# A decoder step on one core: sample state stored by GpSimd, key/value stores a stage later, modulation and last gating beside products, the sample tile in four column quarters

## The reference, cut to what matters

```python
mod = (c @ w_ada + b_ada)[:, None, :]
sh1, sc1, gt1, sh2, sc2, gt2 = jnp.split(mod, 6, axis=-1)
h = x * (1.0 + sc1) + sh1
(qkv_a, z_a, b_a, a_a, q_b, k_b, v_b, f_b, g_a, g_b) = _split_cols(h @ w_in, IN_SIZES)
...
o_a, ssm_new = _gdn_chunked(q_a, k_a, v_a, beta, g, ssm0.astype(f32), chunk)
...
merged = jax.nn.sigmoid(g_a) * (o_a @ w_ba) + jax.nn.sigmoid(g_b) * (o_b @ w_bb)
x = _layernorm(DEEPNORM_ALPHA * x + gt1 * (merged @ w_out), ln1_g, ln1_b)
h2 = x * (1.0 + sc2) + sh2
```

## Time and profile before

| | us |
|---|---|
| median of three runs | 1723.35 |
| lowest, highest | 1720.29, 1732.3 |
| profiled execution | 1724.44 |
| its span | 1722.4 |
| TensorE busy in the span | 1570.8 (91%) |
| VectorE, ScalarE, GpSimd busy | 610.7, 322.2, 300.4 |

### The profile page before, as it was taken

One profiled execution on the slowest core, in us unless ns is written; L12 is line 12 of the kernel. 1 busy time (PEld: TensorE's weight loads), 2 busy tenths in 40 slices (PEclk: granted clock), 3 DMA queues, 4 the chain that ended last, 5 costly groups with the idle time before them and its releaser, 6 DMA issues. The chain is left out here.

```text
span 1722.4 us, 20830 instructions
## 1 busy us (share of the span) xinstructions
PE 1570.8 (91%) x7950; PEld 896.8 (52%) x7950; DVE 610.7 (35%) x1254; ACT 322.2 (19%) x697; POOL 300.4 (17%) x328
## 2 busy tenths in 40 slices
PE   5998999999999995999889978999999999998966
PEld 2865766664467783877764433333433433343422
DVE  2001344343274543442457962331111111111128
ACT  1002222433232221222110210111111111111121
POOL 5000000000018993000000341111111111111100
PEclk9998999999999997999899989999999999999989
DMA  9312110112153214130933026899999999999865
GB/s 337 111 49 83 49 50 1 49 50 80 53 147 132 99 64 133 58 120 16 339 107 127 25 98 258 337 422 416 416 414 405 399 410 412 387 416 421 322 234 247
DMA packets 111678, 357.13 MB, mean 207 GB/s; under 512 B 36011, under 2 KB 36139, under 8 KB 85459
## 3 DMA queue, kind: packets, MB, share of 16 engines
q1 hardware_dynamic: 88582, 304.08, 46.0%
q0 software_dynamic: 14384, 35.89, 5.3%
q10 hardware_dynamic: 8614, 15.84, 2.7%
HBM read 330.70 MB, written 37.64 MB: 214 GB/s over the span
## 5 line engine op out<-in xcount | busy, mean ns | idle before, releaser
L1959 PE MATMUL bank<-arena 128*32 128x512 f32 (+2 forms) x1536 | 334.9, 618 | 27.5 <-DMA arena<-in_w_up 27.5
L1959 PEld LDWEIGHTS bank<-arena 128*32 128x32 f32 (+2 forms) x1536 | 119.6, 138 | 210.3 <-issue 207.7
L1967 PE MATMUL bank<-arena 128*32 128x512 f32 (+2 forms) x768 | 168.7, 598 | 0.7 <-DVE arena L2654 0.7
L2648 DVE TENSOR_TENSOR arena<-arena,bank 128x256 f32<-128x256 f32 x46 | 19.4, 422 | 329.5 <-ACT arena L2323 329.5
L429 PE MATMUL bank<-arena 128*128 128x272 f32 x512 | 123.6, 405 | 8.4 <-PEq L252 4.0
L1172 PE MATMUL bank<-arena 128*128 128x272 f32 x512 | 128.1, 398 | 2.3 <-DMA arena<-in_w_in 2.0
L1946 POOL DMA_INDIRECT expert_rows<-arena x46 | 46.4, 1009 | 480.2 <-PE bank L1952 416.0
L437 PE MATMUL bank<-arena 128*128 128x512 f32 (+4 forms) x384 | 124.3, 482 | 2.8 <-PEq L1744 2.7
L429 PEld LDWEIGHTS bank<-arena 128*128 128x128 f32 x512 | 100.5, 197 | 30.8 <-issue 6.8
L1967 PEld LDWEIGHTS bank<-arena 128*32 128x32 f32 (+2 forms) x768 | 54.9, 134 | 110.7 <-issue 109.8
L1172 PEld LDWEIGHTS bank<-arena 128*128 128x128 f32 x512 | 93.3, 190 | 25.8 <-issue 5.0
(11 more groups left out here) (443 smaller groups left out, 2064.0 us busy)
## 6 DMA issues: line engine op xcount, KB each, us to landing
arena<-in_w_gate SPq DMA_DIRECT2D x64, 1024.0 KB, 12.9
arena<-in_w_up SPq DMA_DIRECT2D x64, 1024.0 KB, 17.8
arena<-in_w_down SPq DMA_DIRECT2D x64, 1024.0 KB, 15.8
arena<-in_w_ada SPq DMA_DIRECT2D x12, 2048.0 KB, 10.4
arena<-in_w_in SPq DMA_DIRECT2D x11, 2048.0 KB, 9.4
arena<-expert_rows SPq DMA_DIRECT2D x8, 2048.0 KB, 26.7
gate_logits<-arena ACTq DMA_DIRECT2D x16, 272.0 KB, 2.8
arena<-gate_logits SPq DMA_DIRECT2D x8, 544.0 KB, 5.6
```

The source lines that it names most:

```text
L1959: mm = nc.tensor.matmul(out[rows].rearrange("p (a n) -> p a n", a=2), x[:, k, rows], gate_up_slot(n)[:, :, k, :], start=k == 0, stop=k == ...
L1967: mm = nc.tensor.matmul(out[rows, :], h[:, k, rows], down_slot(n)[:, k, 512 * half:512 * half + 512], start=k == 0, stop=k == 1)
```

## The change

- GpSimd, no longer SyncE, issues the stores of the sample state and outputs, the eight row moves and the load of branch B's weights, after its own recurrence. SyncE's list goes from slab 3 to slab 11 without a break.
- The six stores of keys, values and log values are issued in the next stage, behind the two history loads.
- `modulate(1)` runs in the projection stage; TensorE starts the first feature group with k = 0 to 3 of both halves, waits for it, and then takes k = 4 to 7.
- The gating of group m = 7 runs at the start of the output projection's stage; TensorE starts tile 0 with k = 0 to 6 of both halves, waits for `mT_last`, and then takes k = 7. ScalarE's load of the gate bias waits for `mT_last` too (it overwrites `ta`).
- The sample tile's values and output projection are 32 products of 128 columns each instead of eight of 512, in four column groups of 32 output partitions; the copies, and the first step of `layernorm`, read four pieces.

Lines that only moved are shown once below.

```diff
@@ -239,7 +239,17 @@
     xT_mm, xT_sb = Tick(nc, "xT_product"), Tick(nc, "xT_copied")
-    const_done = Tick(nc, "constants_done")
+    const_done, hT_done = Tick(nc, "constants_done"), Tick(nc, "tokens_modulated")
+    def modulate(dve, g):
+        step = chained(dve, vch)
+        for kk in range(4 * g, 4 * g + 4):
+            run = hT[:, kk, 0:SEQ]
+            step(nc.vector.tensor_scalar(run, run, modT[:, KD + kk, 0:1], modT[:, kk, 0:1], ALU.mult, ALU.add))
+        seqs = hT[:, 4 * g:4 * g + 4, SEQ:TOK].rearrange("p k (b t) -> p k b t", b=DB)
+        by = lambda k0: modT[:, k0 + 4 * g:k0 + 4 * g + 4, 1:DB + 1].unsqueeze(3).to_broadcast([P, 4, DB, DS])
+        step(nc.vector.tensor_tensor(seqs, seqs, by(KD), ALU.mult))
+        done(hT_done, nc.vector.tensor_tensor(seqs, seqs, by(0), ALU.add))
@@ -384,25 +394,15 @@
-            def modulate(g):
...
             add_bias(0)
             take_modT(1)
-            modulate(0)
+            modulate(dve, 0)
             add_bias(3)
             take_modT(3)
-            modulate(1)
@@ -430,6 +430,15 @@
+    QUARTERS = [(slice(QUAD * q, QUAD * q + QUAD), slice(P * q, P * q + P)) for q in range(4)]
+    def sample_major(out, lhs, w):
+        for k in range(KD):
+            for rows, cols in QUARTERS:
+                mm = nc.tensor.matmul(out[rows, 0:P], lhs[:, k, SEQ:TOK], w[:, k, cols], start=k == 0, stop=k == KD - 1)
+        return mm
     def token_major(out, t, lhs, w, cols, kt=KD):
@@ -446,7 +455,15 @@
             w = arrived(pe, 4)
-            for m in range(CW):
+            for depth in range(2):
+                if depth:
+                    pe.wait_ge(hT_done.sem, 2)
+                for i in range(2):
+                    for k in range(4 * depth, 4 * depth + 4):
+                        mm = nc.tensor.matmul(bank[i][:, 0:HALF], w[:, k, 0:P], hT[:, k, i * HALF:(i + 1) * HALF],
+                                              start=k == 0, stop=k == KD - 1)
+            fq_mm.inc(mm)
+            for m in range(1, CW):
                 mm = feature_major(w, m, hT, bank[2 * m:2 * m + 2])
@@ -461,7 +478,7 @@
                 pe.wait_ge(fk_sb.sem, t // 2 + 1)
-                fv_mm.inc(token_major(bank[t][0:TOKS[t], :], t, hT, w, slice(0, W)))
+                fv_mm.inc(token_major(bank[t].ap(), t, hT, w, slice(0, W)) if t < PT else sample_major(bank[t], hT, w))
@@ -506,17 +523,6 @@
             load_projection(sp, 1)
-            sp.wait_ge(ktm_sb.sem, NT)
...
@@ -527,7 +533,9 @@
                 act.wait_ge(fv_mm.sem, t + 1)
-                fv_sb.inc(nc.scalar.copy(v_tm[0:TOKS[t], t, :], bank[t][0:TOKS[t], :]))
+                for rows, cols in QUARTERS if t == PT else [(slice(0, P), slice(0, W))]:
+                    ins = nc.scalar.copy(v_tm[0:TOKS[t], t, cols], bank[t][rows, 0:cols.stop - cols.start])
+                    ach.inc(ins) if cols.stop < W else fv_sb.inc(ins)
@@ -547,6 +555,7 @@
             step = chained(dve, vch)
+            modulate(dve, 1)
             for m in range(CW):
@@ -601,7 +610,7 @@
     group_at, taken = {}, [0]
-    fox_stored = stored.n
+    fox_stored = stored.n + 6 * 16
@@ -812,6 +821,14 @@
             hist_load.inc(sp.dma_start(hist[NH:NH + CONV, :], A["conv_w"][0]), 16)
+            kp = A["k_prompt"][0, 0].rearrange("(t p) h d -> p t (h d)", p=P)
+            stored.inc(sp.dma_start(kp, k_tm[:, 0:PT, :]), 16)
+            stored.inc(sp.dma_start(A["k_sample"][0].rearrange("b t h d -> (b t) (h d)"), k_tm[0:NS_TOK, PT, :]), 16)
+            vp = A["v_prompt"][0, 0].rearrange("(t p) h d -> p t (h d)", p=P)
+            stored.inc(sp.dma_start(vp, v_tm[:, 0:PT, :]), 16)
+            stored.inc(sp.dma_start(A["v_sample"][0].rearrange("b t h d -> (b t) (h d)"), v_tm[0:NS_TOK, PT, :]), 16)
+            stored.inc(sp.dma_start(A["logf_prompt"][0, 0].rearrange("(t p) h -> p t h", p=P), logf[:, 0:PT, :]), 16)
+            stored.inc(sp.dma_start(A["logf_sample"][0].rearrange("b t h -> (b t) h"), logf[0:NS_TOK, PT, :]), 16)
             for b in range(NKV):
@@ -1307,7 +1324,7 @@
         "w_products", "w1_copied", "w2_copied", "state_read", "u_done", "o_product", "state_updated", "o_copied"))
-    srec, so_back = Tick(nc, "sample_recurrence"), Tick(nc, "sample_out_moved")
+    state_out, so_back = Tick(nc, "sample_state_stored"), Tick(nc, "sample_out_moved")
     t_act, masks_in = Tick(nc, "later_inverse_T_copied"), Tick(nc, "level_masks_in_psum")
@@ -1561,21 +1578,7 @@
                 load_later(sp, j)
-            for j in range(3, 8):
-                send_later(j)
-            sp.wait_ge(srec.sem, 1)
...
-            for j in range(8, len(LATER)):
+            for j in range(3, len(LATER)):
                 send_later(j)
@@ -1616,7 +1619,18 @@
                 sum_keys(so[:, t, :])
-            srec.inc(nc.gpsimd.tensor_copy(skv, so[:, 0, :]))
+            step(nc.gpsimd.tensor_copy(skv, so[:, 0, :]))
+            out = A["ssm_sample"][0].rearrange("b h k v -> (b h) k v")
+            for half in range(2):
+                r = slice(64 * half, 64 * half + 64)
+                state_out.inc(pool.dma_start(out[:, :, 32 * half:32 * half + 32], sS[r]), 16)
+                so_back.inc(pool.dma_start(scr_o.rearrange("b h t d -> (b h) t d")[:, :, 32 * half:32 * half + 32], so[r]), 16)
+            pool.wait_ge(so_back.sem, 32)
+            for b in range(DB):
+                so_back.inc(pool.dma_start(qkv_tm[DS * b:DS * b + DS, PT, 0:W].rearrange("p (h d) -> p h d", h=H),
+                                           scr_o[b].rearrange("h t d -> t h d")), 16)
+            pool.wait_ge(state_out.sem, 32)
+            branch_in[1].inc(pool.dma_start(wbb, A["w_branch_b"][0].rearrange("(k p) n -> p k n", p=P)), 16)
@@ -1823,7 +1837,7 @@
                     tokval_made.inc(nc.vector.tensor_scalar(rows, rows, float(2 * q - QUAD * TOPK * q), None, ALU.add))
-            for m in range(KD):
+            for m in range(KD - 1):
                 dve.wait_ge(sg_done.sem, m + 1)
@@ -1835,6 +1849,7 @@
             sample_token_values()
+            dve.wait_ge(sg_done.sem, KD)
@@ -1852,6 +1867,7 @@
         "h2_done", "h2T_in_psum", "h2T_copied", "logits", "scores_sigmoid"))
+    mT_last = Tick(nc, "last_group_gated")
     h2_store, shw = Tick(nc, "h2_stored"), Tick(nc, "shared_loaded")
@@ -2028,11 +2044,8 @@
                 for half in halves:
-                    if t:
-                        pe.wait_ge(wo_read.sem, 2 * (t - 1) + half + 1)
-                    if t == 0:
-                        pe.wait_ge(wo_in[half].sem, 16)
-                    wo_mm.inc(token_major(bank[half][0:TOKS[t], :], t, mT, wo[half], slice(0, 512)))
+                    pe.wait_ge(wo_read.sem, 2 * (t - 1) + half + 1)
+                    wo_mm.inc(token_major(bank[half].ap(), t, mT, wo[half], slice(0, 512)) if t < PT else sample_major(bank[half], mT, wo[half]))
@@ -2123,7 +2136,16 @@
-            out_rows(0, 0, 1)
+            for depth in (range(KD - 1), range(KD - 1, KD)):
+                if depth[0]:
+                    pe.wait_ge(mT_last.sem, 1)
+                for half in range(2):
+                    if depth[0] == 0:
+                        pe.wait_ge(wo_in[half].sem, 16)
+                    for k in depth:
+                        mm = nc.tensor.matmul(bank[half].ap(), mT[:, k, 0:P], wo[half][:, k, :], start=k == 0, stop=k == KD - 1)
+                    if depth[0]:
+                        wo_mm.inc(mm)
             out_rows(1, 0, 1)
@@ -2247,6 +2269,7 @@
             load_mod(act, gtb, 0, gtb_load)
+            act.wait_ge(mT_last.sem, 1)
             gtb_load.inc(act.dma_start(b_gt, A["b_ada"][0:1, 2 * D:3 * D].broadcast_to([P, D])), 16)
@@ -2450,8 +2473,10 @@
                     dve.wait_ge(wo_mm.sem, 2 * t + half + 1)
-                    cols = slice(512 * half, 512 * half + 512)
-                    done(wo_read, TT(r[:, cols], bank[half][0:n, :], gtb[0:n, t // PT, cols], ALU.mult))
+                    for rows, part in QUARTERS if t == PT else [(slice(0, P), slice(0, 512))]:
+                        cols = slice(512 * half + part.start, 512 * half + part.stop)
+                        ins = TT(r[:, cols], bank[half][rows, 0:part.stop - part.start], gtb[0:n, t // PT, cols], ALU.mult)
+                        vch.inc(ins) if part.stop < 512 else done(wo_read, ins)
                 step(STT(r, x, ALPHA, r, ALU.mult, ALU.add))
@@ -2603,6 +2628,10 @@
+            for out, b, g in ((ta, 2, sg[(KD - 1) % NG][:, 0, :]), (tb, 6, sg[(KD - 1) % NG][:, 1, :])):
+                step(TT(out[:, 0:HALF], bank[b][:, 0:HALF], g[:, 0:HALF], ALU.mult))
+                step(TT(out[:, HALF:TOK], bank[b + 1][:, 0:HALF], g[:, HALF:TOK], ALU.mult))
+            done(mT_last, TT(mT[:, KD - 1, :], ta, tb, ALU.add))
             layernorm(0)
```

28 lines of the change are left out of this document (removed).

## The result

Four runs of the changed kernel gave 1698.21 us in the median (1690.55 to 1704.39), four of the kernel before 1724.48: the ratio is 0.985, 95% interval 0.982 to 0.988, or 26 us. Five later runs, beside eleven of the kernel before (1725.31), had a median of 1693.18 and a ratio of 0.9815 (0.979 to 0.984), 32 us. The forecast was 41.5 us, 1683 with a range of 1672 to 1696. So the direction was right, the size was 10 to 15 us too large, and the first median lies outside the range; the second, 1693.18, lies in its upper half.

What follows compares the result with a forecast made beforehand. TensorE, busy 91% of the span, bounds the kernel before 1020 us; the experts' weights fill the DMA engines after. The terms sum to 41.5 us off 1724.44: 1682.9, say 1683, range 1672 to 1696.

Steps and rivals of the forecast that it cites:

- State stored by GpSimd: TensorE's 18.9 us wait for a slab and the slow clock behind it go: 20.2 us gained (18.5 to 21).
- my price: GpSimd's own transfers: 14 us by the DMA or 73 by the row moved, plus some 10 for two waits.
- Pause at the attention stage: Stores issued a stage later cut TensorE's 6.0 us wait at the stage's start to about 0.5: 5.5 us gained.
- Clock: Attention stage's start: without the idle, TensorE holds 2.4 GHz where it ran at 1.2: 6.5 us gained (0 to 7.9).
- the mixture at 200 to 210: The same mixture of products ran at 2.4 GHz at 200 to 210 us, so it can hold the high clock.
- Rival (a): The clock falls at the start of the attention stage all the same: 1689.5 us, chance 0.24.
- Modulation: Projection stage: VectorE's second modulation runs beside the first eight products, so TensorE starts earlier: 2.95 us gained.
- the values' quarters: Sample tile's values in four overlapping column groups take 2.0 us instead of 7.05: 5.0 us gained.
- The 0.4: Projection stage: the shorter pause keeps part of the half-clock stretch of 43.5 to 48 from happening: 0.4 us gained.
- Quarters in the output projection: Sample tile: VectorE leads and reads eight small pieces instead of two: 1.0 us lost, up to 3 with the clock fallen.
- Last gating: Output projection: the last group's gating runs beside its products, so the stage starts earlier: 2.0 us gained (0.3 to 4).

Runs made afterwards that it cites:

- x15: The changed kernel with the values of the sample tile in one piece again (8 products of 512 columns): ratio 0.982 to the kernel before.
- x8: The changed kernel with the last gating before the end of its stage again and the gate bias loaded without a wait: ratio 0.9818 to the kernel before.

## Why the prediction was too large

- **State stored by GpSimd, 20.2.** Right: 20.8 by the aligned traces, 21 us alone. Also right that GpSimd's transfers are covered, and my price was too high: 24 to 83 us with the waits, measured 17, of which 6.3 are a wait. Each store of 4096 pieces held GpSimd 1.7 to 1.9 us, 0.41 to 0.45 ns a piece and not 7.7.
- **Pause at the attention stage, 5.5.** Right: 5.69 by the aligned traces.
- **Clock, 6.5: this step failed.** I took the mixture at 200 to 210 as proof that the clock holds if the pause goes. It fell 3 to 7 us into the stage in all seventeen traces without the pause, for 3.4 to 10.3 us. The fourth output came 22.3 us after the start in the mean of the three traces with the pause and 20.1 in the mean of the seventeen, 2.2 gained; between the unaltered kernels (two and four traces) it is 0.7. Rival (a) had the mechanism; it put the gain at nothing. The one trace that the forecast was made from had the long slow stretch, so part of the 6.5 was chance.
- **Modulation, 2.95 + 0.4, and the values' quarters, 5.0.** The pause lost 2.98 (4.04 to 1.06), the tile 5.09. Both right in their place; the 5 us of the tile do not show in the median of x15. The 0.4 fits: the clock was low until 4.6 and 4.4 us behind the first product in the two traces of the kernel before, and until 3.6 to 4.2 in the four after, half of which difference is 0.3.
- **Quarters in the output projection, -1.0: mis-sized.** It was -3.0, the end of its own range. VectorE's reads gave the 1.1 that I counted (2.51 for 1.39); TensorE's low clock behind the new 6.4 us of idle gave the rest by the sum (L2094 took 9.03 us for 7.13).
- **Last gating, 2.0.** Right in its place: VectorE's chain, which leads the stage, starts 2.3 us earlier by twenty traces. TensorE then waits 1.92 us for VectorE, as the step itself said. The times alone (x8, 1.6 us) cannot tell it from nothing.
- **The term that was missing: this failed too.** I put the stages between the edits at nothing, without a reason. The DeltaNet stage does change: VectorE and GpSimd collide by phase, the change moves the phase to the edge, and two of four profiles lose 6.6 us. I had looked at the neighbouring case, VectorE against GpSimd's transfers in the earlier trace rows, and not at VectorE against GpSimd's arithmetic, though instructions of one size and 0.69 to 2.7 us stood in the trace of before.
- **One profile as the base.** The forecast subtracts from a single execution whose experts' stage was at the short end of 654.8 to 662.1.

Clock 5.8 (6.5 less the 0.7 of the same traces), output projection 2.0 and phase 3.3 (6.6 in half of the profiles) make 11.1 of the 11.7 us between 41.5 and the means' 29.8. That it comes out so close is luck: single traces of one kernel vary by more, in their spells of slow clock and in the experts' stage.

## What to carry to other kernels

Ask of every edit what it does to the phase between VectorE and GpSimd: in these traces a VectorE instruction with both operands in SBUF ends only 0.55 us behind a long GpSimd instruction that began before it (4.00 us instead of 0.69), and with one operand in PSUM it keeps its 0.69. So put one operand of those on the critical path into PSUM. Cut a short tile into column quarters only where TensorE leads; where VectorE leads it pays for more reads and TensorE comes back slow. A slow stretch behind a pause is not owed to the pause alone: here 3.4 to 10.3 us of 13.7 to 20.5 stayed when the pause was gone. Take more than one profile before the size of a stage goes into a sum.
